# Interleaving the bias matmuls of the spatial gating unit with its main matmuls

## The reference

```python
def chunk_sgu(z, ln_g, ln_b, w_s, b_s):
    z = jax.nn.gelu(z)
    u, v = jnp.split(z, 2, axis=-1)
    v = layernorm(v, ln_g, ln_b)
    B, L, C = v.shape                       # 1, 256, 256
    vg = v.reshape(B, L // SGU_CHUNK, SGU_CHUNK, SGU_GROUPS, C // SGU_GROUPS)
    mixed = jnp.einsum('gpq,bnqgc->bnpgc', w_s, vg) + b_s.T[:, :, None]
    return u * mixed.reshape(B, L, C)
```

## Time and profile before

| what | value |
|---|---|
| median of 3 runs | 2452.69 us (2452.64, 2452.69, 2457.8) |
| profiled execution | 2452.69 us, span 2450.6 us |
| mean granted TensorE clock | 0.942 of full speed |
| TensorE busy | 2192.9 us, 89% |
| VectorE busy | 1122.5 us, 46% |
| ScalarE busy | 886.6 us, 36% |

### The profile page before, as it was taken

One profiled execution on the slowest core, in us unless ns is written; L12 is line 12 of the kernel. 1 busy time (PEld: TensorE's weight loads), 2 busy tenths in 40 slices (PEclk: granted clock), 3 DMA queues, 4 the chain that ended last, 5 costly groups with the idle time before them and its releaser, 6 DMA issues. The chain is left out here.

```text
span 2450.6 us, 45037 instructions
## 1 busy us (share of the span) xinstructions
PE 2192.9 (89%) x19466; PEld 1767.7 (72%) x19466; DVE 1122.5 (46%) x1982; ACT 886.6 (36%) x1491; POOL 51.1 (2%) x94
## 2 busy tenths in 40 slices
PE   7998798998786999889999998877888998898999
PEld 7967465665463997767777776644777998777999
DVE  5355335433432743543333333523755555756554
ACT  5444232233211543332222222332444444544443
POOL 0000000000000000000000000000000000000001
PEclk9999899998898999999999999987998999988999
DMA  7494899999999567759999999898413554413551
GB/s 265 155 335 173 348 418 394 411 406 401 398 403 376 174 205 258 283 192 366 406 402 404 400 423 411 359 395 314 135 58 121 190 166 159 147 55 121 179 174 61
DMA packets 138928, 676.27 MB, mean 276 GB/s; under 512 B 10592, under 2 KB 10848, under 8 KB 76512
## 3 DMA queue, kind: packets, MB, share of 16 engines
q1 hardware_dynamic: 130048, 614.77, 65.5%
q0 software_dynamic: 8672, 58.50, 6.0%
HBM read 672.17 MB, written 1.05 MB: 275 GB/s over the span
## 5 line engine op out<-in xcount | busy, mean ns | idle before, releaser
L463 PE MATMUL bank<-xx,high 128*128 128x256 f32 (+1 forms) x3296 | 632.6, 293 | 35.6 <-DVE xx L624 22.5
L463 PEld LDWEIGHTS bank<-xx,high 128*128 128x128 f32 (+1 forms) x3296 | 523.1, 194 | 90.3 <-issue 60.6
L463 PE MATMUL bank<-xx,low 128*128 128x256 f32 (+1 forms) x1648 | 474.7, 288 | 0.0
L463 PEld LDWEIGHTS bank<-xx,low 128*128 128x128 f32 (+1 forms) x1648 | 320.9, 195 | 1.4
L412 DVE TENSOR_TENSOR low<-lane,high 128x1024 fp32r<-128x1024 f32 (+1 forms) x112 | 130.7, 1170 | 306.4 <-ACT high L401 306.4
L401 ACT ACTIVATE high<-lane 128x1024 fp32r<-128x1024 f32 (+1 forms) x112 | 113.1, 1014 | 296.0 <-PE bank L463 296.0
L463 PE MATMUL bank<-hx,high 128*128 128x256 f32 x1056 | 197.1, 288 | 0.0
L463 PEld LDWEIGHTS bank<-hx,high 128*128 128x128 f32 x1056 | 164.1, 191 | 16.1 <-issue 15.2
L463 PE MATMUL bank<-hx,low 128*128 128x256 f32 x528 | 149.0, 282 | 0.0
L1438 ACT ACTIVATE hs<-bank 64x256 f32<-64x256 f32 x64 | 24.1, 377 | 284.8 <-PE bank L1425 284.7
L1445 DVE TENSOR_TENSOR hs<-hs,bank 64x256 f32<-64x256 f32 x64 | 27.1, 423 | 204.8 <-ACT hs L1438 204.3
(11 more groups left out here) (557 smaller groups left out, 4027.2 us busy)
## 6 DMA issues: line engine op xcount, KB each, us to landing
ring__15<-in_expert_gu_blocks SPq DMA_DIRECT2D x52, 1024.0 KB, 9.5
ring__14<-in_expert_gu_blocks SPq DMA_DIRECT2D x51, 1024.0 KB, 10.0
ring__16<-in_expert_gu_blocks SPq DMA_DIRECT2D x51, 1024.0 KB, 10.0
ring__50<-in_expert_gu_blocks SPq DMA_DIRECT2D x26, 1024.0 KB, 9.7
ring__16<-in_expert_down_blocks SPq DMA_DIRECT2D x26, 1024.0 KB, 8.4
ring__14<-in_expert_down_blocks SPq DMA_DIRECT2D x26, 1024.0 KB, 9.2
ring__146<-in_expert_gu_blocks SPq DMA_DIRECT2D x26, 1024.0 KB, 10.0
ring__49<-in_expert_gu_blocks SPq DMA_DIRECT2D x25, 1024.0 KB, 10.2
```

The lines of the kernel that those rows point to most:

```text
L463: done = pe.matmul(out, a.bitcast(F32R), b.bitcast(F32R), start=it["start"] and k == 0 and q == 0 and not halves, stop=stop)
```

## The change

The bias matmuls no longer come first for both chunks. Each main matmul is followed by a bias matmul of 128 columns into the same part of the bank, at another tile position. The main matmul now starts the sum and the bias ends it. The wait for `shift` moves to the head of the helper.

```diff
             def sgu_pe(pe, cs):
+                pe.wait_ge(*sgu_v.at(K("shift")))
                 for c in cs:
                     bank = take(pe, bk, K("sgu", c))
-                    for g in (2 * c, 2 * c + 1):
-                        q0 = 64 * (g % 2)
-                        rows = bc(R("sgub", 512 * L + g * P, P)[0].bitcast(F32), [2, 2, P], 1)
-                        pe.matmul(bank[q0:q0 + 64, 0:T], ones[96:98, 0:64], rows, start=True, stop=False, tile_position=(96, q0))
-                    pe.wait_ge(*sgu_v.at(K("shift")))
                     for a in range(2):
                         for g in (2 * c, 2 * c + 1):
                             q0 = 64 * (g % 2)
-                            n = pe.matmul(bank[q0:q0 + 64, a * P:(a + 1) * P], sv[:, a, g * 64:(g + 1) * 64], wst[:, g, :], start=False, stop=a == 1,
-                                          tile_position=(0, q0))
+                            o = bank[q0:q0 + 64, a * P:(a + 1) * P]
+                            pe.matmul(o, sv[:, a, g * 64:(g + 1) * 64], wst[:, g, :], start=True, stop=False, tile_position=(0, q0))
+                            n = pe.matmul(o, ones[96:98, 0:64], R("sgub", 512 * L + g * P, P)[0].bitcast(F32), start=False, stop=True,
+                                          tile_position=(96, q0))
                     n.then_inc(*sgu_p.up(K(c)))
```

## The result

The changed kernel takes 2471.35 us (median of 6 runs, 2466.17 to 2473.38) against 2452.66 us for the kernel before (6 runs). The ratio is 1.007, 95% interval 1.0054 to 1.0088. The medians lie 18.7 us apart, where 7.6 were forecast. The forecast was 2460.3 with a range up to 2466.0, so the direction was right and the size was not. The profiled execution took 2472.62 us, its span 2470.8, which is 20.2 more than the span before.

A forecast was written before the change was run, and what follows sets the result against it. It took the query-stream helper calls on TensorE to stand on the chain of waits: four calls at 1.72 (6.88) plus 0.76 in the context stream make 7.6 us, added to 2452.69 for 2460.3 us; range 2455.0 to 2466.0.

The forecast's parts named there:

- Where it counts: Four query-stream helper calls stand on the chain of waits and pass their loss on in full: 6.9 us.
- The price per matmul: In the helper, each lone 128-column matmul costs 0.15 + 0.21 = 0.36 us; eight cost 2.88 per call.
- Rivals 1 and 3: In the helper: half the switches overlap, 2455.3 us, chance 0.10; or switches free and halves independent, 2452.1, chance 0.05.
- Changes of shape against lost pairing: Split of each helper call's added time: six more changes of shape at 0.15 are 0.9, the rest lost pairing.
- the 1.72: Added us per helper call: 2.88 after the change against 1.16 before.
- The early wait: The wait on `shift` at the helper's head costs nothing, as the value was there for over 10 us.
- rival 2: Clock falls to half in the query streams: 2.65 us per place, 2465.6 total; 0.12 together with all six calls on the path.
- the stretch of L1006: Evidence against a clock fall: a block of 8 records in one half of the array kept its pace.
- the full cost of all calls: All six helper calls on the path at 2.2 us each: 13.3 us, 2466.0; 0.12 together with the clock.
- The upper bound: 2466.0 us, from a dearer block price read at the 2x128 bias of L465, with all six calls on the path.
- the 0.06 per block: Possible extra per helper block over 0.15, from 0.19 plus some 0.09 at L465; 0.5 more per call.
- The context stream: Idle of 1.56 and 1.12 us covers its two calls partly; 0.16 and 0.60 us late, 0.76 charged.

The follow-up runs named there:

- biases-together: Kernel before, but in the query stream both calls' bias matmuls come before the first main one; 2450.25 us, ratio 0.9999.
- 128-row: Kernel before, but the bias matmul has the main one's tile shape, with a 128x64 table as weights and the same result; 2450.63 us, ratio 0.9991.
- pairs kernel: The change, but for each chunk both main matmuls and then both bias ones; 2451.53 us, ratio 0.9979 against the kernel before.
- context-only kernel: The change in the two context-stream calls only, the kernel before's order in the query streams; 2455.43 us, ratio 1.0009.
- split kernel: The change, but the second query-stream call comes two projection items later, with dense matmuls between; 2465.56 us, ratio 1.0029 against the kernel before.
- grouped: The change's matmuls without alternation: per call four main together, then four bias together; 2448.24 us, ratio 0.9981 against the kernel before.
- same shape: The change's order, but bias matmuls use 128 rows of ones and zeros at the main position, leaving out the bias; 2447.83 us, ratio 0.9982.

## Why the forecast was wrong, point by point

- **Where it counts.** Right: the four query-stream calls lie on the chain and cost in full, 15.9 us in the trace, and 15.3 by the medians of the runs with these calls only.
- **The price per matmul.** Right to the hundredth at full clock: 0.36 us per matmul, 2.88 per call, taken from single starts. The biases-together and the 128-row kernels confirm its two parts. Rivals 1 and 3 needed records of different shapes to start together; none did.
- **Changes of shape against lost pairing.** Only the price of a change is borne out: the pairs kernel has two more blocks per call than before and takes 0.30 us more, 0.15 for each. That 0.8 us per call are lost pairing is what remains of the 1.72 and was not measured by itself.
- **The early wait.** Right: no wait on `shift` appears, and the 1.02 us of idle time before each context call were there before the change too.
- **The clock: the step that failed.** I set rival 2 at 2.65 us per place and gave it, with another case, a chance of 0.12. It came at both places and cost 4.6 each, 9.2 us, half of the whole result. Two things were wrong. The evidence that I set against it did not bear: that "no idle gap is added" only says that waits are not the cause, the 60% of streaming did not keep the clock, and the stretch of L1006 was 1.02 us long, while the clock fell 3.1 us after the helper's first record. And the price was that of one stretch of 5.3 us at the lower level, taken at another place. The fall came during the helper, whose second call then took 4.7 us instead of 2.9, and the lower level lasted 10.2 us. The low clock makes the thin stretch longer, 7.6 us instead of 5.8.
- **The range.** I put the clock and the full cost of all calls beside each other as alternatives, each reaching 2466. They add up. 2460.3 plus 9.2 is 2469.5, within 2 us of the median. The upper bound itself was badly worked out: 0.19 and 0.09 are two changes of shape, 0.14 us each and thus no more than my 0.15; the 0.06 per block does not follow from them.
- **The context stream.** I charged 0.76 us, with the clock held or even helped. In the trace of the change this is wrong too. Timeline of the changed kernel, and of the kernel before at its second call:

```profile
411.58 0.49 PE L437 MATMUL bank<-xx,zeros 128*128 128x512 f32 x1
...
425.96 0.40 PE L2297 MATMUL bank<-wst,tm 128*64 128x128 f32 x2 [1.02 <-ACT kt L2210]
...
429.83 3.78 PE L1339 MATMUL bank<-d_t,xn 128*128 128x128 f32 x16
...
434.60 0.49 PE L437 MATMUL bank<-xx,zeros 128*128 128x512 f32 x1
```

```profile
428.73 0.65 PE L2295 MATMUL bank<-row,vec 2*64 2x256 f32 x4 [1.02 <-ACT kt L2210]
```

The idle before L437 is gone at both calls, as forecast. From the helper's first record to L437 the first call took 5.1 us, as before. The second took 434.60 - 425.96 = 8.64 us against 433.77 - 428.73 = 5.04, 3.6 more where I had 0.60: the clock fell here too, 1.4 us after the helper's first record and for 6.8 us, and L1339 took 3.78 us instead of 2.05. With the 15.9 us of the query streams that is 19.5 of the 20.2 us between the traces. In the context-only kernel both calls lost clock, 4.7 us together, and in the split kernel, which has the change's order here, both again, 4.7. So five of the six context calls in these three kernels saw the clock fall during the helper or within 0.5 us of its end. With the order of before, or with one shape, L1339 took 2.05 us at all fourteen calls of seven kernels. The pairs kernel lost clock at its first call as well (L1339 3.63 us); in the grouped one the level was low before its first call began. How much of the 3.6 us reaches the end of the program is not settled, as this stage also waits for transfers (L1425 for 1.98 us at 462 us) and drifts by several us between runs; the medians of the context-only kernel are 2.1 us above before.

Three kernels without long lone alternation (grouped, pairs, same shape) came out 0.2% below before, with intervals that touch or nearly touch 1. The reason is open.

## What to carry to other kernels

In these kernels matmuls at different positions of the array shared it only as long as the tile shape stayed the same. Group them by shape, or give the small one the shape of its neighbours; a 128-row bias matmul full of zeros was cheaper here than one of 2 rows (1.88 us a pair of calls instead of 2.33), though by too little to show in the total. And when a change makes TensorE's work thinner without an idle gap, price the clock as a term of its own that adds to the others: the low level also stretches the thin part and the dense work behind it.

## What was unexpected of the hardware

The granted clock fell to 0.50 without any wait on TensorE, 3.1 us after the first record of the alternation at both places of the query streams, while each record of the engine's line in the trace still followed the last without a gap (busy 2.88 of 2.88 us). A stretch of 6.07 us with dense matmuls in it kept 1.00. With 4.0 us of helper the clock fell at one place of two. The 3.1 us are no property of the alternation: in the second context call the clock fell after 1.4 us, and in the pairs and split kernels 0.5 and 0.4 us after the helper had ended. At the layer 0 place of the change it had come back to 1.00 only 3.7 us before the helper. And main and bias matmuls that alternate in program order run two abreast by themselves when the shape is the same: 0.98 us per call.
